# Moving the pooling group's mixing product ahead of a projection in the TensorE order of a streaming encoder

## The reference

```python
h = _rmsnorm(x, norm_g)
u = jnp.einsum('btd,de->bte', h, w_in)
a_b, a_c, a_x, a_g, b_v, b_a, b_g, c_u, c_g, x_q, x_g = jnp.split(u, N_SPLITS, axis=-1)
y_a = a_b * _dwconv(pad(a_c * a_x), conv_a_w) * silu(a_g)            # 3 taps
z = _layernorm(_dwconv(pad(b_v * sigmoid(b_a)), conv_b_w) + bias)    # 31 taps
y_b = silu(z) * silu(b_g)
d = multiscale_trailing_mean(c_u) - c_u
mixed = jnp.einsum('btgc,gce->btge', d, pool_w) + pool_bias          # the product "mix"
y_c = mixed * pool_scale * silu(c_g)
y_x = softmax(q k / 8) v * silu(x_g)                                 # 4 heads, 256 memory tokens
out = rmsnorm(x + concat(y_a, y_b, y_c, y_x) @ w_out)
```

## Time and profile before

| | |
|---|---|
| median of three runs | 1518.89 us (1517.99 to 1519.69) |
| profiled execution, its own time | 1519.69 us |
| its span in the trace | 1517.8 us |
| TensorE busy | 1436.0 us, 95% of the span |
| VectorE busy | 1106.7 us, 73% |
| ScalarE busy | 554.8 us, 37% |
| GpSimd busy | 239.8 us, 16% |
| mean granted clock of TensorE | 0.984 of full speed |

### The profile page before, as it was taken

One profiled execution on the slowest core, in us unless ns is written; L12 is line 12 of the kernel. 1 busy time (PEld: TensorE's weight loads), 2 busy tenths in 40 slices (PEclk: granted clock), 3 DMA queues, 4 the chain that ended last, 5 costly groups with the idle time before them and its releaser, 6 DMA issues.

```text
span 1517.8 us, 32241 instructions
## 1 busy us (share of the span) xinstructions
PE 1436.0 (95%) x11758; PEld 1231.4 (81%) x11758; DVE 1106.7 (73%) x2950; ACT 554.8 (37%) x1159; POOL 239.8 (16%) x188
## 2 busy tenths in 40 slices
PE   5878999999999999999999999999999999999955
PEld 4767888888888888888888888888888888888843
DVE  6997776949587676959587675949587685949572
ACT  7774332423234332433234232333233232323231
POOL 2252110111111110111111101111111111111100
PEclk9989999999999999999999999999999999999978
DMA  9977536355544537355644626454644626454525
GB/s 269 247 287 205 175 89 240 87 186 165 174 166 138 193 79 230 106 166 173 186 166 112 220 69 217 128 166 166 193 158 106 234 69 203 142 159 167 161 100 175
DMA packets 216418, 253.22 MB, mean 167 GB/s; under 512 B 139593, under 2 KB 165373, under 8 KB 216381
## 3 DMA queue, kind: packets, MB, share of 16 engines
q1 hardware_dynamic: 216381, 252.74, 53.0%
HBM read 193.62 MB, written 26.05 MB: 145 GB/s over the span
## 4 chain that ended last, share of the span: by engine, by line
PE 47%; DVE 25%; issue 13%; DMA 8%; ACT 3%; SPq 1%; DVEq 1%; POOL 1%; ACTq 0%; POOLq 0%
DVE z L1213 10%; PE u L456 8%; PE u L458 8%; PE u L457 8%; DMA pt<-prow 6%; PE sps L456 4%; PE sps L458 4%; PE sps L457 4%; PE qps L456 4%; PE qps L458 4%; PE qps L457 4%; DVE prow L1240 2%; DVE xb L1149 2%; ACT probs L844 2%; DVE st L1221 1%
## 5 line engine op out<-in xcount | busy, mean ns | idle before, releaser
L456 PE MATMUL u<-h_hi,w_hl 128*128 128x256 f16 (+1 forms) x2992 | 792.1, 270 | 10.6 <-DVE w_hl L1195 8.5
L457 PE MATMUL u<-h_lo,w_hl 128*128 128x256 f16 (+1 forms) x2992 | 791.3, 270 | 0.0
L458 PE MATMUL u<-h_hi,w_hl 128*128 128x256 f16 (+1 forms) x2992 | 790.9, 270 | 0.0
L1213 DVE SCALAR_TENSOR_TENSOR z<-glu,cst,z 128x256 f32<-128x256 f32 (+1 forms) x1020 | 425.4, 487 | 1.3 <-issue 0.3
L456 PEld LDWEIGHTS u<-h_hi,w_hl 128*128 128x128 f16 x2992 | 294.5, 99 | 56.7 <-issue 12.0
L458 PEld LDWEIGHTS u<-h_hi,w_hl 128*128 128x128 f16 x2992 | 294.5, 99 | 33.7
L457 PEld LDWEIGHTS u<-h_lo,w_hl 128*128 128x128 f16 x2992 | 294.5, 99 | 32.5
L759 ACT ACTIVATE gate<-u,inv 128x256 f32<-128x256 f32 (+1 forms) x204 | 83.1, 458 | 172.4 <-PE u L458 172.2
L844 ACT ACTIVATE probs<-sps,st 128x256 f32<-128x256 f32 (+1 forms) x132 | 60.7, 471 | 151.7 <-DVE st L1221 151.6
L456 PE MATMUL sps<-ring,y_hi 128*128 128x512 f32 (+1 forms) x280 | 111.8, 399 | 3.8 <-DVE y_lo L1250 2.5
L1556 DVE TENSOR_TENSOR ob<-sps,ob 128x512 f32<-128x512 f32 (+1 forms) x33 | 21.3, 686 | 128.4 <-PE sps L458 128.4
(11 more groups left out here) (203 smaller groups left out, 1794.7 us busy)
## 6 DMA issues: line engine op xcount, KB each, us to landing
ring<-wo_split SPq DMA_DIRECT2D x264, 512.0 KB, 6.0
ob<-in_x_prompt SPq DMA_DIRECT2D x34, 512.0 KB, 4.2
out<-ob SPq DMA_DIRECT2D x32, 512.0 KB, 3.5
w_hl<-in_w_in SPq DMA_DIRECT2D x20, 512.0 KB, 7.3
wo_split<-ring SPq DMA_DIRECT2D x16, 512.0 KB, 4.7
xb<-in_x_prompt SPq DMA_DIRECT2D x15, 512.0 KB, 6.6
probs<-in_x_prompt SPq DMA_DIRECT2D x15, 512.0 KB, 3.3
rows<-in_w_out SPq DMA_DIRECT2D x16, 256.0 KB, 5.2
```

The source lines that it names most:

```text
L456: nc.tensor.matmul(out, a_hi, b_hi, start=first, stop=False)
L457: nc.tensor.matmul(out, a_hi, b_lo, start=False, stop=False)
L458: return nc.tensor.matmul(out, a_lo, b_hi, start=False, stop=last)
L1213: ins = nc.vector.scalar_tensor_tensor(z[:, c, 0:n], glu[:, c, k:k + n], w, z[:, c, 0:n], ALU.mult, ALU.add)
```

## The change

In the list of bank turns and in TensorE's order, `mix` moves from behind `attend` 1 to ahead of the projection b_g. ScalarE's order follows: it reads `mix` ahead of b_g. In SLOTS the two entries b_g and mix change places, so that mix takes the bank that a_x used and b_g takes the bank that a_b used. Before, b_g took the bank of a_x and mix that of a_b. Chunk 0 keeps its order (`first_chunk` and the list FIRST are as before). No instruction is added or taken away.

```diff
-SLOTS = ["b_a", "b_v", "x_q", "c_u", "a_c", "a_x", "a_b", "a_g", "b_g", "mix", "c_g", "x_g", "zf",
+SLOTS = ["b_a", "b_v", "x_q", "c_u", "a_c", "a_x", "a_b", "a_g", "mix", "b_g", "c_g", "x_g", "zf",
          "zb"]
@@ tensor engine, chunk()
                 project(i, n, "a_b")
                 attend(i, n, 0)
                 project(i, n, "a_g")
+                mix(i, n)
                 project(i, n, "b_g")
                 attend(i, n, 1)
-                mix(i, n)
                 project(i, n, "c_g")
                 project(i, n, "x_g")
                 z_rows(i, n)
@@ scalar engine, chunk()
                 probs_hi(i, n, 1)
                 d_high(i, n)
                 scaled_out(i, n, "a_g", gate[:, 2, :, 0:n], ACT.Silu, ag_ok)
+                mixed(i, n)
                 b_gate(i, n)
-                mixed(i, n)
                 y_high(i, n, 0, ya[:, :, 0:n], ya_ok)
```

## The result

The changed kernel takes 1535.55 us (median of four runs, 1534.61 to 1536.86) against 1519.29 us for the kernel before: ratio 1.0109, 95% interval 1.0091 to 1.0127. It is 16.3 us slower; the prediction had +15.7 and 1534.6 us. The profiled execution took 1536.11 us, with a span of 1534.3.

The account below looks back on a forecast made before the run. TensorE's own order bounds the kernel. Per chunk +1.89 us less a hole of 0.85 gives +1.04; 15 chunks, the sample at 0, sum to +15.7 on 1519.69; less 0.80 for the median, 1534.6 us, 8 in 10 for 1530 to 1538.5.

Parts of the forecast that it names:

- What bounds: Full chunks: TensorE's own order sets the time, 95% busy; VectorE starts each chunk on b_v; +1.04 us a chunk.
- absorbed in part: Rival: an unseen slack, a later TensorE wait that shrinks, gives back +4 to +12, 1523 to 1531 us; chance 0.06.
- `mix` waits for `d_low`: Behind a_g: `mix` stands about 0.96 us for dq_lo, which comes at T + 6.23, and starts at T + 6.29.
- b_g waits for `ab_out` by the turn of the banks: Behind `mix`: b_g writes a_b's bank, which `ab_out` reads until T + 7.82, so it starts at T + 7.96.
- the bank is no wait: Rival: only dq_lo holds `mix`, b_g has no bank wait; +0.25 us a chunk, +3.8, 1522.7 us; chance 0.04.
- `attend` 1 doesn't wait any more: Behind b_g: probabilities landed at T + 11.41, so `attend` 1 starts at T + 13.29 without a wait.
- the hole: TensorE's standstill ahead of `attend` 1, waiting for transposed probabilities; averages 0.85 us a chunk, 0.87 gained in chunk 7.
- ScalarE's order costs nothing: ScalarE, `mixed` ahead of `b_gate`: through by T + 14.2, before `y_high` of ya starts at 728.84; no cost.
- The sample at 0, +-0.3: Sample's chunk: `attend` 0 waits 20.15 us, the same products stand in another order; 0, bounds -0.3 and +0.3.
- The gain: Rival: both VectorE results in time, only the hole is filled; -0.77 us a chunk, -11.6, 1507.3 us; chance 0.05.
- The clock: Rival: two standstills a chunk drop TensorE to half clock for 3.3 us; 25 us more, 1559 us; chance 0.05.

Follow-up runs that it names:

- own_bank: Changed kernel with `mix` writing a bank that only the output projection uses and b_g given a_x's bank back: 1525.33 us, ratio 1.0030 to the kernel before.
- ab_first: Changed kernel with VectorE's `ab_out` moved ahead of the tap pair that stood before it, banks as changed: 1524.79 us, ratio 1.0030.
- sample_old_order: Changed kernel with only the sample's chunk (64 tokens) put back in the old order, on ScalarE too: 1534.12 us, ratio 1.0098.
- early_both: Changed kernel with VectorE's and ScalarE's orders altered so that `d_low` and `ab_out` come ahead of `probs_lo` 1: 1507.76 us, ratio 0.9919.
- wait_alone: Kernel before with one wait added, nothing moved: TensorE waits for the end of `ab_out` ahead of b_g: 1562.19 us, ratio 1.0281.
- wait_split: Kernel before with TensorE waiting for `ab_out` ahead of b_g and also for `d_low` ahead of a_g's last three products: 1561.7 us, ratio 1.0285.
- mix_then_attend: Kernel before with `mix` and `attend` 1 changed round in TensorE's order alone (a_g, b_g, mix, attend 1, c_g): 1505.86 us, ratio 0.9909.

## Why the prediction was right, point by point

1. **What bounds.** TensorE's order sets the time, and VectorE starts each chunk on b_v: held. The 15 changed chunks take from the first `glu_out` at 168.03 to the sample's at 1469.83, 1301.80 us, where before it was 1286.76: +15.04, 1.00 a chunk against +1.04 predicted. So the rival "absorbed in part" falls too: what chunk 7 loses between a_g and c_g (13.99 us against 13.05) its period loses as well (86.85 against 85.88). Two slips stand in the prediction's working: 15 x 1.04 is 15.6 and not 15.7, and b_g starts 2.7 us later than before, not 2.6 (T + 7.96 against T + 5.25; T is a_g's first start). Neither moves the forecast by more than 0.1 us.

2. **`mix` waits for `d_low`.** Predicted a standstill of 0.96 us and a start at T + 6.29; measured 0.96 in chunk 7 and T + 6.38. From VectorE's end to `mix` it took 0.15 us and not the 0.06 taken from another product; it changes nothing, as b_g behind it waits longer.

3. **b_g waits for `ab_out` by the turn of the banks.** Predicted T + 7.96, measured T + 7.87: the 0.08 us that I added for a first load that can't come ahead isn't there. Its wait is 0.55 us a chunk, where about 0.7 was forecast. This step decides: without it the loss is 5 us (own_bank, ab_first), with it 16. The rival "the bank is no wait", 1522.7 us, is what these two kernels came to, 1525.3 and 1524.8 by the medians; against their own runs of the kernel before they lose 5.0 and 4.5 us where +3.8 was worked out, and 4.3 us each from chunk 1's `glu_out` to the sample's.

4. **`attend` 1 doesn't wait any more, and the hole is gained.** Held: its wait for the DMA is gone, and it starts 0.20 us after b_g's last product.

5. **ScalarE's order costs nothing.** Held: its `y_high` of ya waits for VectorE as before, behind `mixed` and `b_gate` (1.41 us in chunk 7; 1.31 before).

6. **The sample at 0, +-0.3.** This step failed. In the first profile the sample lost 2.2 us, 2.0 of them between `attend` 0 and c_g, where the clock came back later than before. The same products in another order are not the same work when a part of it runs at half clock. `mix` now stands in the stretch before the clock's return and takes 1.29 us, the first two lines below; in the kernel before it stood behind that return and took 0.70, the last two:

```profile
1502.51 0.40 PE L456 MATMUL u<-dq_hi,pw_hi 128*128 128x64 f32 x1
...
1503.80 0.26 PE L456 MATMUL u<-h_hi,w_hl 128*128 128x64 f16 x1
```

```profile
1490.15 0.30 PE L456 MATMUL u<-dq_hi,pw_hi 128*128 128x64 f32 x1
...
1490.85 0.20 PE L456 MATMUL u<-h_hi,w_hl 128*128 128x64 f16 x1
```

The rest, 1.4 us, is the later return itself, whose cause stays open (sample_old_order). Chunk 0, whose order is unchanged, was 0.8 us shorter. That is scatter: chunk 1's first `glu_out` starts anywhere from 166.8 to 170.8 us in the 13 profiles, all with the same order in chunk 0. 15.0 + 2.2 - 0.8 makes up the 16.5 us between the two spans, but for rounding. So the chunks fell 0.7 us short of the predicted 15.7 and the sample and chunk 0 put 1.4 on top. The mechanism of the chunks held step by step, whatever the total; that the total came so near is in part luck.

7. **The rivals.** The gain is real where both results come early: early_both gains 12.5 us on its own runs of the kernel before, where 11.6 was worked out. The clock stayed at 1.00 in the changed kernel's full chunks, though wait_alone and wait_split show how near that rival was: at 2.3 to 2.7 us of standing in a chunk, in place of 1.5, it came into force in 9 or 10 of 15 chunks.

## What to carry to other kernels

Before an instruction is moved up in an engine's order, look up the end of each thing that it waits for, and then who takes over its old place in a turn of buffers: here the second wait was of a projection that wasn't moved, and it made two thirds of the loss. Work put into a hole should go just ahead of the late wait, where its own inputs are ready (mix_then_attend, -0.9%), and not a whole projection earlier. And where TensorE is the bound, a wait may cost more than its length.

## What the runs showed of the hardware that was not expected

- After a chunk's standstill of 2.44 us in one piece (wait_alone, chunk 7), or of 1.24 and 1.08 us with three products between (wait_split), TensorE's granted clock was at 0.50 (1.2 GHz) for about 3 us, in 10 and 9 of 15 chunks, and stayed at 1.00 in the others, all but one of which had the same standstill (chunk 15 had 0.4 us less). After 0.96 and 0.55 us with `mix` between, it never fell, in the five profiles of the changed kernel and of those with the sample's old order. The Trainium skill, in "TensorE: Matmul & The Clock Gate", section "Why this matters for your kernels", ties a drop in the middle of a kernel to one long idle gap between bursts of matmuls. The runs don't agree that the one gap decides: where the longest was 1.19 us the clock fell in chunk 6 of wait_split, with 1.08 us to follow, and stayed in chunk 1 of the changed kernel, with 0.55 to follow.
- After the sample's standstill of about 19 to 20 us the clock came back 2.8 us after `attend` 0 in one profile (before) and after 7.9 in another (changed), for the same products but six.
- The first float32 product behind a row of float16 ones starts 0.03 us after the last of them (715.99, 716.02), and the second 0.20 us after the first (716.22, mix_then_attend).
- At full clock a float32 product of `mix` takes 0.12 us from start to start with 256 columns (724.75, 724.87 in the changed kernel) and as much with 64 (1490.28, 1490.39 in the kernel before). A float16 product takes 0.109 us with 256 columns and 0.03 with 64 (1488.41, 1488.44). So `mix` costs 0.7 us in the sample too, at a quarter of a full chunk's columns.
